# Last down projection by columns and quarters, key matrix in quarters, sigmoids by Tanh, in a two-layer decoder kernel with a mixture of experts

## The reference

```python
def hgrn2_mixer(h, ...):                      # layer 0
    q, f_logit, i, g = split(h @ w_in)
    f = lb + (1.0 - lb) * sigmoid(f_logit)    # forget gate; k = 1 - f
    o = gated_linear_recurrence(q, 1 - f, i, log(f))
    return (rms_norm(o, o_norm) * silu(g)) @ w_out

def hier_moe(h, ...):                         # both layers
    hu = xb @ w_in[e]                         # 1024 -> 2 x 512, per expert
    y  = (silu(hu[:, :512]) * hu[:, 512:]) @ w_out[e]     # 512 -> 1024

for layer in range(2):
    x = x + mixer(rms_norm(x))                # layer 0: HGRN2; layer 1: attention
    x = x + hier_moe(rms_norm(x))
    if layer == 0:                            # shared keys and values from x
        k, v = split(rms_norm(x, kv_norm) @ w_kv)
```

## Time and profile before

| | |
|---|---|
| median of 3 runs | 1170.19 us (1170.01 to 1170.5) |
| the profiled execution, its own time | 1170.16 us |
| its span, first to last instruction | 1168.3 us |
| TensorE busy | 867.6 us (74%) |
| VectorE busy | 359.9 us (31%) |
| ScalarE busy | 131.4 us (11%) |
| HBM read | 444.41 MB, 383 GB/s over the span |

### The profile page before, as it was taken

The page is one execution under the profiler, slowest core; times in us unless marked ns, Lnnn a source line. Parts: engine busy times, 40 slices in busy tenths (PEclk is TensorE's granted clock), DMA queues, the critical chain, the costliest instruction groups (busy, mean ns, idle before and its releaser), DMA issues.

```text
span 1168.3 us, 12565 instructions
## 1 busy us (share of the span) xinstructions
PE 867.6 (74%) x5238; PEld 415.8 (36%) x5238; DVE 359.9 (31%) x549; ACT 131.4 (11%) x320; POOL 22.9 (2%) x27
## 2 busy tenths in 40 slices
PE   9999998946665656656689999996565757565767
PEld 7965655312221212222234565532222222222222
DVE  4978874010202020202048746402020202020203
ACT  1112211100000000000011251110000000000000
POOL 1000100000000000000002100000000000000000
PEclk9999999987778787878899999997788787878789
DMA  9994588999999999999999837799999999999997
GB/s 350 303 317 194 216 328 312 425 429 428 427 428 429 428 428 429 428 425 429 415 411 404 367 144 296 297 426 429 428 428 426 429 427 430 427 428 425 429 418 291
DMA packets 51818, 447.77 MB, mean 383 GB/s; under 512 B 4496, under 2 KB 6840, under 8 KB 26936
## 3 DMA queue, kind: packets, MB, share of 16 engines
q1 hardware_dynamic: 49696, 444.42, 91.9%
q10 hardware_dynamic: 2072, 2.62, 1.2%
HBM read 444.41 MB, written 2.62 MB: 383 GB/s over the span
## 4 chain that ended last, share of the span: by engine, by line
DMA 45%; PE 45%; SPq 5%; issue 2%; DVE 2%; ACT 1%; POOL 0%; DVEq 0%
PE ps L1387 44%; DMA ring<-in_moe_w_in 29%; DMA ring<-in_moe_w_out 15%; SPq L462 3%; SPq L368 2%; DMA ring<-in_w_kv 1%; PE ps L1390 1%; DMA xs<-const_turned 0%; ACT work L633 0%; DVE work L1128 0%; DVE work L1267 0%; SPq L496 0%; DVE work L1218 0%; DVE xs L843 0%; DVE work L910 0%
## 5 line engine op out<-in xcount | busy, mean ns | idle before, releaser
L1387 PE MATMUL ps<-ring,work 128*32 128x512 f32 (+1 forms) x3360 | 599.7, 691 | 249.5 <-DMA ring<-in_moe_w_in 150.3
L1387 PEld LDWEIGHTS ps<-ring,work 128*32 128x32 f32 (+1 forms) x3360 | 191.1, 135 | 598.1 <-issue 584.9
L1204 DVE TENSOR_SCALAR work<-work 128x512 f32<-128x512 f32 x16 | 6.8, 427 | 658.0 <-ACT work L691 658.0
L1387 PE MATMUL ps<-work 128*128 128x128 f32 (+4 forms) x498 | 126.7, 437 | 3.1 <-ACT work L698 1.6
L1387 PEld LDWEIGHTS ps<-work 128*128 128x128 f32 (+2 forms) x498 | 64.3, 176 | 63.7 <-issue 61.2
L633 ACT ACTIVATE work<-ps,first 128x128 f32<-128x128 f32 x120 | 34.2, 367 | 274.1 <-PE ps L1387 274.1
L1387 PEld LDWEIGHTS ps<-work,xs 128*128 128x128 f32 x512 | 58.7, 192 | 13.7 <-issue 13.4
L1387 PE MATMUL ps<-work,xs 128*128 128x128 f32 x512 | 62.4, 279 | 0.0
L1390 PE MATMUL ps<-first,work 128*128 128x128 f32 x160 | 25.6, 308 | 41.5 <-DVE work L1213 38.9
L698 ACT COPY work<-ps 128x512 f32<-128x512 f32 x32 | 18.7, 585 | 318.0 <-PE ps L1387 318.0
L1206 DVE RECIPROCAL work<-work 128x512 f32<-128x512 f32 x16 | 53.6, 3353 | 0.6
(11 more groups left out here) (159 smaller groups left out, 394.1 us busy)
## 6 DMA issues: line engine op xcount, KB each, us to landing
ring<-in_moe_w_in SPq DMA_DIRECT2D x112, 2048.0 KB, 20.0
ring<-in_moe_w_out SPq DMA_DIRECT2D x50, 2048.0 KB, 20.0
ring<-in_moe_w_in SPq DMA_DIRECT2D x22, 1024.0 KB, 15.9
ring<-in_hg_w_in SPq DMA_DIRECT2D x7, 2048.0 KB, 20.9
ring<-in_moe_w_out SPq DMA_DIRECT2D x24, 512.0 KB, 14.1
work<-in_moe_w_out SPq DMA_DIRECT2D x4, 2048.0 KB, 9.9
ring<-in_moe_w_in SPq DMA_DIRECT2D x12, 512.0 KB, 7.6
ring<-in_w_kv SPq DMA_DIRECT2D x3, 2048.0 KB, 24.7
```

Source lines behind the costliest of these rows:

```text
L1387: return pe.matmul(o, l, r, start=start, stop=stop)
```

## The change

- `sigmoid(x)` is made as (1 + tanh(x/2))/2. ScalarE does Tanh in place of Exp. In the expert quads VectorE does two SCALAR_TENSOR_TENSOR instructions in place of an add, a reciprocal and two products; in the mixer the add and the reciprocal of all eight pieces go.
- The last quad's down matrices come in six parts: row blocks 0 and 1 whole; blocks 2 and 3 of the left columns; block 2 of the right columns; block 3 of columns 512 to 768; block 3 of columns 768 to 1024. The right half is multiplied in two quarters, in banks 7 and 5.
- The residual and the sum over the first seven quads are added before the last quad's `combine` (`add_most`), which then starts its banks anew. The last quad's share is added in three column pieces for each token tile (`add_last`): 512, 256 and 256 wide.
- The key matrix comes in four quarters of 1 MB, the two left ones first.
- The output goes out in six DMAs in place of four. Some semaphores are merged.

```diff
+LAST_DOWN = [(slice(0, 1), slice(0, D)), (slice(1, 2), slice(0, D)), (slice(2, KF), slice(0, 512)),
+             (slice(2, 3), slice(512, D)), (slice(3, KF), slice(512, 768)), (slice(3, KF), slice(768, D))]
+LAST_COLUMNS = [slice(0, 512), slice(512, 768), slice(768, D)]
+LAST_BANKS = [(0, 2), (1, 3), (7, 2)]
...
             experts(0)
             c = MIX1
-            for i, w in enumerate((w_kv[:, 0:D], att_w_q[0], w_kv[:, D:2 * D], att_w_o[0])):
...
+            for half in range(2):
                 for j in range(2):
...
+                    if half == 0:
+                        sp.wait_ge(*read(c + j - RING))
+                    sp.dma_start(quarter(c, j, half), rows_of(w_kv[:, 0:D], j)[:, :, half * 512:(half + 1) * 512])\
+                      .then_inc(loaded[(c + j) % RING] if half else key_part_in[j], 16)
...
-                        act.activation(en, ps[:, 6, :], ACT.Exp, scale=-1.0).then_inc(exp_done, 1)
+                        act.activation(en, ps[:, 6, :], ACT.Tanh, scale=0.5).then_inc(exp_done, 1)
...
+                        if last_quad(it, u):
+                            act.wait_ge(down_done, it * (2 * UN) + (2 * q + 1))
+                            act.wait_ge(c_done, it * (4 * UN) + 4 * q)
+                            act.copy(y[:, 0:512], ps[:, 6, :]).then_inc(y_ready, 1)
+                            act.wait_ge(quarter_down, layer + 1)
+                            act.copy(y[:, LAST_COLUMNS[1]], ps[:, 7, 0:256]).then_inc(quarter_y, 1)
+                            act.wait_ge(down_done, it * (2 * UN) + (2 * q + 2))
+                            act.copy(y[:, LAST_COLUMNS[2]], ps[:, 5, 0:256]).then_inc(y_ready, 1)
+                            continue
...
-                    dve.tensor_scalar(en, en, 1.0, None, ALU.add).then_inc(silu_step, 1)
-                    dve.wait_ge(silu_step, it * (3 * UN) + (3 * q + 1))
-                    dve.reciprocal(en, en).then_inc(silu_step, 1)
-                    dve.wait_ge(silu_step, it * (3 * UN) + (3 * q + 2))
-                    dve.tensor_tensor(en, en, ps[:, 6, :], ALU.mult).then_inc(silu_step, 1)
-                    dve.wait_ge(silu_step, it * (3 * UN) + (3 * q + 3))
+                    dve.scalar_tensor_tensor(en, en, 1.0, ps[:, 6, :], ALU.add, ALU.mult).then_inc(silu_ready, 1)
+                    dve.wait_ge(silu_ready, it * UN + (q + 1))
...
+                        part_in(2)
+                        down(group(r), 0, range(2, KF)).then_inc(down_done, 1)
+                        pe.wait_ge(most_added, 2 * layer + 2)
+                        for a in range(TT):
+                            combine(it, u, a, 0, True, True)
+                        part_in(3)
+                        last_quarters(group(r), [2])
+                        meanwhile()
+                        part_in(4)
+                        down(group(r), 1, [KF - 1], 7, 0).then_inc(quarter_down, 1)
+                        pe.wait_ge(quarter_y, layer + 1)
+                        for a in range(TT):
+                            combined(LAST_BANKS[1][a], a, LAST_COLUMNS[1], True, True).then_inc(quarter_c, 1)
                         group_in(r)
-                        down(group(r), 1, [KF - 1]).then_inc(down_done, 1)
-                        combine(it, u, 1, 0, False, True)
+                        down(group(r), 1, [KF - 1], 5, 256).then_inc(down_done, 1)
+                        pe.wait_ge(y_ready, it * (2 * UN) + (2 * q + 2))
+                        pe.wait_ge(moe_added, TT * (len(LAST_COLUMNS) * layer + 1))
                         for a in range(TT):
-                            meanwhile(a)
-                            combine(it, u, a, 1, False, True)
+                            combined(LAST_BANKS[2][a], a, LAST_COLUMNS[2], True, True).then_inc(c_done, 1)
```

More of the change, by code:

```diff
@@ L188, in build @@
         rb_in = sem("rel_bias_in")
-        key_part_in = sem("first_key_rows_in")
+        key_part_in = [sem(f"key_rows{j}_first_columns_in") for j in range(2)]
         extra_in = [sem(f"extra_slot{i}_loaded") for i in range(EXTRAS)]
@@ L233, in build @@
         out_done = sem("out_done")
-        ov = [{n: sem(f"over{l}_{n}") for n in ("w", "wd", "shift", "picked", "pick", "gat", "xg", "st", "sp", "up", "exp",
-                                                "silu", "hid", "ht", "hidT", "y", "ye", "c", "x", "back",
-                                                "end")}
+        ov = [{n: sem(f"over{l}_{n}") for n in ("w", "shift", "picked", "pick", "gat", "xg", "turned", "sp", "products",
+                                                "exp", "silu", "hid", "hidT", "ye", "c", "x", "back", "end")}
               for l in range(2)]
@@ L455, in load_last_down @@
                     r = QC * UN - GRP
-                    parts = [(k, slice(0, D)) for k in range(KF - 1)] + [(KF - 1, slice(0, 512)), (KF - 1, slice(512, D))]
-                    for i, (k, cs) in enumerate(parts):
+                    for i, (ks, cs) in enumerate(LAST_DOWN):
                         for x in range(GRP):
@@ L572, in _ @@
                     act.wait_ge(f_done, hp + 1)
-                act.activation(part, part if hp < 2 else ps[:, heads_bank(0, hp), :], ACT.Exp, scale=-1.0).then_inc(f_exp, 1)
+                act.activation(part, part if hp < 2 else ps[:, heads_bank(0, hp), :], ACT.Tanh, scale=0.5).then_inc(f_exp, 1)
                 if hp == 2:
@@ L601, in _ @@
                 if kind:
-                    act.activation(gate[:, i % 2, half], ps[:, 4 + l % 4, :], ACT.Exp, scale=-1.0).then_inc(g_exp, 1)
+                    act.activation(gate[:, i % 2, half], ps[:, 4 + l % 4, :], ACT.Tanh, scale=0.5).then_inc(g_exp, 1)
                 else:
@@ L1025, in _ @@
             tile_sums(hT, four_sums(7), 0)
-            forget_reciprocal(2)
             forget_and_keys(2)
@@ L1379, in _ @@
             moe(1)
-            for half in range(2):
-                add_experts(1, half)
+            for n in range(len(LAST_COLUMNS)):
+                add_last(1, n)
         @block.tensor
@@ L1628, in hidden_T, with down @@
                 i.then_inc(signal, 1)
-            def down(weights, half, ks):
+            def down(weights, half, ks, bank=None, lo=None):
+                bank, width = (6 + half, 512) if bank is None else (bank, 256)
+                cs = slice(half * 512 + (lo or 0), half * 512 + (lo or 0) + width)
                 for k in ks:
@@ L1633, in down @@
                         rows = slice(x * BLK, (x + 1) * BLK)
[L1634 to L1635 removed]
+                        i = mm(ps[rows, bank, 0:width], hidT[:, k, rows], down_view(weights[x])[:, k, cs], k == 0, k == KF - 1)
                 return i
@@ L1800, in body @@
                                 for a in range(TT):
-                                    combine(it, u, a, half, first, False)
+                                    combine(it, u, a, half, first, is_int(it, ITERS - 1))
                             continue
-                        for k in range(KF - 1):
-                            pe.wait_ge(down_part_in[k], 16 * GRP * (layer + 1))
-                            for half in range(2):
-                                down(group(r), half, [k])
-                        pe.wait_ge(down_part_in[KF - 1], 16 * GRP * (layer + 1))
@@ L1808, in body, with part_in @@
-                        down(group(r), 0, [KF - 1]).then_inc(down_done, 1)
-                        combine(it, u, 0, 0, False, True)
+                        def part_in(i):
+                            pe.wait_ge(down_part_in[i], 16 * GRP * (layer + 1))
+                        for k in range(2):
+                            part_in(k)
+                            down(group(r), 0, [k])
+                            last_quarters(group(r), [k])
+                        part_in(2)
+                        down(group(r), 0, range(2, KF)).then_inc(down_done, 1)
@@ L1824, in columns_T @@
                 i.then_inc(nt_done, 1)
-            moe(0, lambda a: columns_T(0, a))
+            moe(0, lambda: [columns_T(0, a) for a in range(TT)])
             def heads_transposes(src, bank0, n0):
```

186 lines of the change are left out of this document (102 added, 84 removed).

## The result

| kernel | median of its runs | range | ratio to before, 95% interval |
|---|---|---|---|
| before | 1170.18 us | 1169.98 to 1170.64 (8 runs) | |
| changed | 1173.39 us | 1170.66 to 1174.71 (8 runs) | 1.0023 [1.0014, 1.0032] |

The change costs 0.23%. The forecast was 1169.4, the range ended at 1171.8: the prediction missed. Note the spread: eight runs of the kernel before lie within 0.7 us, eight of the changed one are spread over 4. The medians differ by 3.2 us, and the ratio, which is taken between runs side by side, amounts to 2.7.

A forecast was written before the change was run, and what follows sets the result against it. The prediction took the kernel as bound by DMA reads at about 428 GB/s, plus two lags and the end. From 1170.16 us it took 0.2 for the tail, 0.45 for the keys and a little for Tanh: 1169.4, range 1167.2 to 1171.8.

The forecast's parts named there:

- Tanh for Exp: Mixer and expert quads: VectorE loses over 80 us of busy time, but worth 0, at most 0.3 us per layer.
- TensorE idles about 2.6 us in place of 0.54: Last quad: `down` begins some 1.7 us sooner, but row blocks 2 land as before, so the gain becomes waiting for DMA.
- the clock rival: Ahead of the third part: longer idling lowers TensorE's clock, 1.4 or 1.7 us lost per fall; chance 18%.
- the 0.65 us forecast for the tail and the keys: Program's end and layer 0's keys: 0.2 us less in the tail and 0.45 us gained at the keys.
- The rival's case "in both": Third part of both layers: the clock falls in each, adding 3.3 us to 1169.4, so 1172.7 us; within the 18%.
- Tanh elsewhere: Mixer, a layer's first quad and the quads' steady part: Tanh takes Exp's time on ScalarE and gains zero.
- The tail of layer 1: Last quad to program's end: VectorE's last add stays at 1165.9, smaller output pieces save 0.2 us: -0.2 us.
- The rival of quarters at the price of halves: Quarter sets in each layer's last quad: four sets on the path cost 0.43 us more each, +3.4, 1172.8 us; 8%.
- Layer 0 and the keys, -0.45: Layer 0's end: the second key product starts at 611.95 in place of 612.39, a gain of 0.45 us.
- VectorE's difference: Third key product: difference of the first slot's halves, 2.28 us; sum ready at 614.5, wanted at 615.4, cover 0.9 us.
- The landing: Last down loads: 2.7 and 3.0 us behind the third part, layer 1's last at 1161.2, hidden by 1.9 us.
- The rival that only the landing would bound the tail: Layer 1's tail: shorter turns over ScalarE leave the last landing as bound, 1.9 us sooner, 1167.2 us in all; 12%.

The follow-up runs named there:

- e9: Changed kernel with 24 products of ones in place of 12 ahead of the last `up` half and 12 more ahead of the third down part: 1170.44 us.
- e3: Changed kernel with Exp, the reciprocal and two products back in the expert quads: 1171.20 us, ratio to before 1.0002.
- e12: Changed kernel with 24 products of ones in place of 12 ahead of the last `up` half, and nothing else: 1174.14 us, ratio to before 1.0032.
- e13: Kernel before with Tanh and without reciprocals in the mixer alone: 1170.21 us, ratio to before 0.9996.
- e7: Kernel before with the key matrix in four quarters of columns, the left ones first: 1170.25 us, ratio to before 0.9995.
- e10: Changed kernel with fills of ones in both idle stretches and the last quarter's `down` ahead of the first quarter's `combine`: 1169.28 us, ratio to before 0.9992.
- e1: Changed kernel with 12 more products of ones ahead of the third down part in each layer's last quad: 1171.86 us, ratio to before 1.0010.

## Why the prediction was wrong

The step that failed is the last quad's in "Tanh for Exp": "TensorE idles about 2.6 us in place of 0.54", with "Tanh's whole worth: 0". And with it the 18% for the clock rival, whose price for each fall was right. What the runs showed in its place: 3.49 us of idling, and 1.6 us lost behind it in each layer. Apart from it, the 0.65 us forecast for the tail and the keys did not come either: without a late fall the kernel takes what it took before (e9, 1170.44 beside 1170.43).

- **Where 2.6 came from.** I took the end of the ones products, 589.44, from the earlier trace rows and put the earlier `down` behind it, at 590.9. But that row stands behind an `up` half of 5.02 us, which had a clock fall in it; I used that very row to price the rival, and not to ask when TensorE arrives without one. At full clock (3.64) the half ends 1.4 us sooner, `down` comes at 589.24, and TensorE idles 3.49. That is close to the 3.56 behind which before shows a fall.
- **The clock.** 16 products took 3.52 and 3.48 us in place of 1.92, 1.6 in each layer; forecast 1.4 to 1.7 (the 1.7 was read from a window that begins 1.55 us before the products do, so it priced some idle time too). A late fall struck in both layers of the first profiled execution and in neither of the second. The rival's case "in both", 1172.7, lies between the medians of 1173.39 and 1172.11, but partly by luck: it stands on 1169.4, 0.8 below what the kernel takes without late falls. Shown by e3 (less idling, same parts), e9 (little idling) and the distance between e9 and e12.
- **Tanh elsewhere.** ScalarE's instruction took 0.60 us, as with Exp. Nothing in the mixer (e13), nothing in the first quad (`hidden_T` there starts at 201.60, still after 1.23 us of waiting for ScalarE, as in the earlier trace rows), nothing in the steady part (428 GB/s from 203 to 560 us in both). Right.
- **The tail of layer 1.** In the second profiled execution it took 1168.6 - 1155.57 = 13.0 us, as before; forecast -0.2. TensorE's part was summed rightly. One, two and three quarter sets took 0.64, 1.07 and 1.50 us, so 0.43 a set and 0.21 for the pipe, as taken; ScalarE's copy of 256 columns took 0.37 against 0.39, its turn 0.49 against 0.62, and two `combine` of 256 columns 1.06 against 0.86, which makes up for it. The last add ended at 1165.09 + 0.85 = 1165.94, forecast 1165.9. The output is the term with the wrong sign: put at 0.2 less, a guess, it took 2.66 us from the last add to the end of the span, against 2.40 before. All eight traces with six output DMAs have 2.66 to 2.97 there, the five with four 2.40 to 2.47. What in the six costs it, no run shows.
- **The rival of quarters at the price of halves** (+3.4) falls: 8 products of 256 columns took 0.64 us, of 512 columns 1.06, and each further set added 0.43 against 0.86.
- **Layer 0 and the keys, -0.45.** The second key product started at about 612.3 in that execution (forecast 611.95; before 612.39): from the landing it took 15.2 us in place of the 14.95 summed, with 0.1 to 0.2 more at most changes from one kind of product to the next, and 0.13 less at each wait for ScalarE. The third product found VectorE's sums ready. I named VectorE's difference as the next to be late; it was its chain some products later that was (line 1353), which releases a weight load at 622.75, and TensorE's 100 products there took 43.34 us against 43.08 in e9. From its third part at 597.08 to ScalarE's first gather of the next experts at 746.52 it took 149.44 us; before, 149.63 from block 2: with the 0.24 that the part lands later the gain is nil. e7 and e10 show the stop openly, 0.40 and 0.91 us of waiting for VectorE.
- **The landing.** Behind the third part no wait of TensorE for a down matrix stands in any trace with the six parts. In e10 the last quarter is multiplied without a wait, its set starting about 1160.38 + 24/32 x 1.93 = 1161.8, 6.0 us behind the third part's landing; the forecast was 5.7 for the two loads behind it, so the last took 3.3 at most beside its neighbour's 2.7. By the price that I worked out from the 64 KB figure of the Trainium skill (DMA: Bandwidth & Descriptors, section Bandwidth), 7.6 us for the last alone, a wait would have stood there; the bound of 3.3 leaves room for the 3.1 from its 1 MB figure, though each DMA was of 128 KB. The page's table was measured on loads that GpSimd issued, and these came from SyncE. The rival that only the landing would bound the tail falls with e10: a shorter chain made it 1.25 us shorter.

What stays open: the highest run of the changed kernel, 1175.57, is 5.3 us over its lowest, more than two falls of 1.6. About 0.9 of that lies outside its span (1172.8 us); but other runs of it have spans up to 1173.1, 4.6 over the shortest. None such was profiled, so a longer fall (an `up` half was lengthened by up to 2.9 us), or a third place, isn't excluded. How often each case comes isn't measured, since only two executions of the changed kernel were profiled. And why the clock falls behind one stretch and not behind its equal isn't settled by any run here.

## What to carry to other kernels

Before a producer off the critical path is made faster, work out how long its consumer will then stand idle, from a row without a clock fall in it as well as from one with; if that wait grows near to a length behind which the trace has shown a fall, the faster producer may cost the time that it saves nowhere. Fill such stretches all or none: here a fill behind one that was left open got in the way when the clock fell at the first, and a fill of the first alone did not mend the loss. And when a time spreads much more than that of its neighbour, take a second profile before explaining the first.

## What the runs showed of the hardware

- Whether the clock falls is not fixed by the idle time: behind 3.45 us it stayed and behind 3.46 it fell in one execution (e12); the last `up` half behind 3.5 us took 3.64, 5.34 and 6.28 us in executions of one program. The Trainium skill (TensorE: Matmul & The Clock Gate, section What's actually happening) says that the point at which the clock rises behind a kernel's start varies from run to run. What varies here is the fall behind idle time, which that sentence doesn't speak of. The same section puts the cost of the rise at the start at under 1% of a typical kernel's span; the two falls here cost 3.2 of 1171.7 us, 0.27%, as small a share, and still the whole result.
- When it falls differs too. In half-microsecond windows the granted clock reached 0.50 ahead of the products in one place (layer 0 of before: at 581.0, the products at 581.55) and behind their start in another (the changed kernel's second profiled execution: at about 582.2, the products at 581.47), which goes with the different lengths of the `up` half.
- A fall is free or costly by its place. The early one lengthens the `up` half by 1.4 to 2.9 us (5.02; e13, 6.58), and where TensorE would have idled ahead of the third part anyway it costs nothing; where a fill took that idle time (e1) it cost about 1.5 us in each layer. The late one adds 1.6 on the path.
- Float32 products of 32 rows: a further set of 256 columns adds 0.43 us, one of 512 columns 0.86.
